# A decoder block with 32 experts on one core: down weights in two transfers, choice rows read by tile and choice, tap products ahead of state products

## What is computed

```python
D_MODEL, SEQ, N_EXPERTS, EXPERT_TOP_K, D_EXPERT = 1024, 512, 32, 2, 512
SSM_WIDTH, SSM_GROUP_DIM, SSM_STATE = 512, 16, 64        # 32 groups, 64 states each

h = rmsnorm(x, norm_mix_g); proj = h @ w_in
ya = pool_mixer(proj[..., :a_end]); yb = sgu_mixer(proj[..., a_end:b_end])
yc = s5_mixer(proj[..., b_end:c_end])
    # states = associative_scan of a complex diagonal recurrence
    # y = einsum('blgp,gcp->blgc', states, c).real + d_skip * u; gelu; gated by sigmoid(y @ glu_w)
x = x + sum(gates * (ys @ w_branch)) @ w_out
t = rmsnorm(x, norm_ffn_g)
...
for e in range(N_EXPERTS):
    y = (silu(t @ w_gate[e]) * (t @ w_up[e])) @ w_down[e]
    out = out + combine[:, e:e + 1] * y                  # two experts of a token are not zero
return rmsnorm(x + out, norm_final_g)
```

## Time and profile before

| what | us |
|---|---|
| median of 3 runs | 930.88 |
| lowest, highest | 930.44, 931.03 |
| the profiled execution | 932.56 |
| its span, first to last instruction | 930.9 |
| PE busy | 835.0 (90%) |
| DVE, ACT, POOL busy | 323.2, 195.7, 142.1 |

### The profile page before, as it was taken

How to read it: one execution, slowest core, us unless ns; L and a number is a source line. 1 busy time by engine, 2 the same in 40 slices (tenths; PEclk the granted TensorE clock), 3 DMA queues, 4 the chain that set the end, 5 groups by cost and what they waited for, 6 DMA issues and landing times.

```text
span 930.9 us, 15236 instructions
## 1 busy us (share of the span) xinstructions
PE 835.0 (90%) x5300; PEld 569.9 (61%) x5301; DVE 323.2 (35%) x604; ACT 195.7 (21%) x289; POOL 142.1 (15%) x239
## 2 busy tenths in 40 slices
PE   7999999999999999989889998899999887777850
PEld 6888888868876888885555554555555444343420
DVE  4899996731524246265101111110101101010106
ACT  5633353222432233141000000000000000000002
POOL 4341601000000000012122221122112121212100
PEclk9999999999999999999999999999999999999995
DMA  8693224523224945049999999999999999999926
GB/s 263 148 186 111 75 66 44 167 69 113 91 90 153 401 148 225 1 160 387 402 417 420 418 418 420 421 420 419 418 420 419 419 420 421 420 420 420 410 118 268
DMA packets 77949, 261.22 MB, mean 281 GB/s; under 512 B 29260, under 2 KB 30284, under 8 KB 53300
## 3 DMA queue, kind: packets, MB, share of 16 engines
q1 hardware_dynamic: 71508, 249.91, 71.1%
q0 software_dynamic: 6256, 10.75, 3.1%
q10 hardware_dynamic: 144, 0.02, 0.0%
HBM read 254.76 MB, written 14.42 MB: 289 GB/s over the span
## 4 chain that ended last, share of the span: by engine, by line
PE 71%; SPq 15%; DVE 5%; DMA 4%; issue 2%; ACT 1%; POOL 0%; DVEq 0%; POOLq 0%; ACTq 0%
PE ps L1009 35%; PE ps L436 17%; SPq L421 14%; PE ps L449 9%; DMA au<-in_exp_w_up 4%; PE ps L994 3%; PE ps L986 1%; SPq L461 1%; PE ps L442 1%; DVE pair L655 1%; DVE pair L650 1%; DVE cv L700 1%; PE ps L1120 1%; PE ps L1148 1%; PE ps L1150 1%
## 5 line engine op out<-in xcount | busy, mean ns | idle before, releaser
L436 PE MATMUL ps<-ssm,pair 128*64 128x256 f32 x1120 | 127.2, 381 | 20.2 <-DMA ssm<-in_exp_w_gate 8.9
L650 DVE TENSOR_TENSOR pair<-pair,ps 128x256 f32<-128x256 f32 x32 | 13.5, 421 | 358.5 <-PE ps L436 358.5
L436 PEld LDWEIGHTS ps<-ssm,pair 128*64 128x64 f32 x1120 | 81.3, 137 | 71.1 <-issue 28.5
L1009 PE MATMUL ps<-h_hi,w_hi 128*128 128x512 f32 x280 | 109.6, 392 | 0.0
L1427 DVE TENSOR_TENSOR w_lo<-raw,w_hi 128x1024 fp32r<-128x1024 f32 x56 | 71.3, 1274 | 110.3 <-ACT w_hi L1236 109.5
L1009 PE MATMUL ps<-h_hi,w_lo 128*128 128x512 f32 x280 | 109.0, 389 | 0.0
L1009 PE MATMUL ps<-h_lo,w_hi 128*128 128x512 f32 x280 | 108.9, 389 | 0.0
L1236 ACT CAST w_hi<-raw 128x1024 fp32r<-128x1024 f32 x59 | 61.8, 1050 | 193.2 <-PE ps L1009 193.2
L714 ACT COPY late<-ps 128x512 f32<-128x512 f32 x35 | 20.5, 586 | 317.5 <-PE ps L449 317.5
L793 POOL DMA_INDIRECT choice_rows<-late,put_now x35 | 35.7, 1021 | 319.9 <-ACT late L714 284.1
L1009 PEld LDWEIGHTS ps<-h_hi,w_hi 128*128 128x128 f32 x280 | 52.6, 188 | 11.2 <-issue 0.4
(11 more groups left out here) (319 smaller groups left out, 1099.1 us busy)
## 6 DMA issues: line engine op xcount, KB each, us to landing
ssm<-in_exp_w_gate SPq DMA_DIRECT2D x22, 2048.0 KB, 29.4
au<-in_exp_w_up SPq DMA_DIRECT2D x11, 2048.0 KB, 30.0
ssm<-in_exp_w_up SPq DMA_DIRECT2D x11, 2048.0 KB, 33.7
ssm<-in_exp_w_down SPq DMA_DIRECT2D x11, 2048.0 KB, 33.9
hl<-in_exp_w_down SPq DMA_DIRECT2D x11, 2048.0 KB, 29.8
raw<-in_w_in SPq DMA_DIRECT2D x40, 512.0 KB, 3.8
hh<-in_exp_w_gate SPq DMA_DIRECT2D x10, 2048.0 KB, 28.4
mb<-in_exp_w_up SPq DMA_DIRECT2D x10, 2048.0 KB, 30.8
```

What stands on the lines that cost most here:

```text
L436: t = nc.tensor.matmul(ps[CAP * h:CAP * (h + 1), bank, 0:HALF], rows[:, k], w[:, k, HALF * h:HALF * (h + 1)], start=k == 0, stop=k == KD - 1)
L650: nc.vector.tensor_tensor(act_cols, silu_cols, up_now, ALU.mult).then_inc(act_ready, 1)
L1009: t = nc.tensor.matmul(bank, lhs, rhs, start=k == 0 and n == 0, stop=k == 2 * count - 1 and n == 2)
```

## The change

Four things, and a tidying that makes room for their semaphores.

1. The down weights of every expert are two transfers of 1 MB, rows `[:, 0]` and `[:, 1]` of the buffer, with a semaphore each (`ew_in[w]["down"]`, `down_rest_in[w]`). `down` waits for the second between its fourth and its fifth matmul. The weights of "over" stay one transfer.
2. Ahead of the four reads of choice rows, the wait for the last scatters comes after the two counter loads and the branch. The four reads of 1 MB are eight of 512 KB, by tile and choice, and VectorE waits for each.
3. For the experts that stand outside the loop, `first_put` waits for its copy first and for the result last, without a `sem_inc` between the last wait and the scatter.
4. In the state-space outputs, the eight tap matmuls of a bank come first, then its sixteen state matmuls.
5. `done2[kind]` and `ov_done[kind]` are one semaphore each, which counts three products for a block.

```diff
-            eng.dma_start(dst, src).then_inc(signal, 16)
+            if signal is ov_w or kind != "down":
+                eng.dma_start(dst, src).then_inc(signal, 16)
+            else:
+                for h, half_in in enumerate((signal, down_rest_in[w])):
+                    eng.dma_start(dst[:, h], src[:, h]).then_inc(half_in, 16)
...
-        def down(w_, bank):
+        def down(w_, bank, pe=None, rest=0):
+
             w = slot_h[EW[w_]["down"]]
             for n, (h, j) in enumerate((h, j) for h in range(2) for j in range(2)):
+                if n == 2 and pe is not None:
+                    pe.wait_ge(down_rest_in[w_], rest)
                 for c in range(2):
...
                     sp.wait_ge(done[kind], e - SETS + 1)
-                    sp.wait_ge(done2[kind], flag + before + 1)
+                    sp.wait_ge(second_done, before * 3 + flag * DONE[kind] + 3)
                     sp.sem_inc(passed, 1)
                     weights(sp, w, kind, e, ew_in[w][kind])
...
-            for w in range(SETS):
-                sp.wait_ge(res_stored[w], USES[w] * 16)
             flag, before = second_of(sp, NE - 1)
             sp.wait_ge(second_rows, (flag + before) * 16 + 16)
             sp.sem_inc(passed, 1)
             with sp.If(n > 0):
                 sp.wait_ge(ov_res_stored, n * 16)
                 sp.sem_inc(passed, 1)
+            for w in range(SETS):
+                sp.wait_ge(res_stored[w], USES[w] * 16)
             for i in range(NT):
-                sp.dma_start(picked_rows(i), res_d.rearrange("(t r) n -> t (r n)", r=4)[i * P:(i + 1) * P, :]).then_inc(picked[i], 16)
+                for c in range(2):
+                    sp.dma_start(picked_rows(i)[:, D * c:D * (c + 1)],
+                                 res_d.rearrange("(t c h) n -> t c (h n)", c=2, h=2)[i * P:(i + 1) * P, c]).then_inc(picked[i][c], 16)
...
             for i in range(NT):
-                v.wait_ge(picked[i], 16)
                 for c in range(2):
+                    v.wait_ge(picked[i][c], 16)
...
-                gp.wait_ge(res_ready, e + 1)
-                put(res[b], e + 1, res_stored[b], put_copied, b)
+                if isinstance(e, int):
+                    gp.wait_ge(put_copied, e + 1)
+                    gp.wait_ge(res_ready, e + 1)
+                    put(res[b], None, res_stored[b], put_copied, b)
...
-                for q in range(4 * i, 4 * i + 4):
-                    outs = [bank[S * two:S * (two + 1), P * (q % 4):P * (q % 4 + 1)] for two in range(2)]
-                    halves = [slice(S * two, S * (two + 1)) for two in range(2)]
+                halves = [slice(S * two, S * (two + 1)) for two in range(2)]
+                outs = [[bank[rows, P * n:P * (n + 1)] for rows in halves] for n in range(4)]
+                for n in range(4):
                     for two in range(2):
-                        nc.tensor.matmul(outs[two], u8v[:, two * Q + q], toep[:, two * Q + q], start=True, stop=False)
-                    for two, rows in enumerate(halves):
-                        nc.tensor.matmul(outs[two], st_re[rows, q], cp_re[rows, q, 1:J + 1].rearrange("p j c -> p (j c)"), start=False, stop=False)
-                    for two, rows in enumerate(halves):
-                        t = nc.tensor.matmul(outs[two], st_im[rows, q], cp_im[rows, q, 1:J + 1].rearrange("p j c -> p (j c)"), start=False, stop=True)
+                        g = two * Q + 4 * i + n
+                        nc.tensor.matmul(outs[n][two], u8v[:, g], toep[:, g], start=n == 0, stop=False, skip_group_check=True)
+                for n in range(4):
+                    q = 4 * i + n
+                    for z, cp in ((st_re, cp_re), (st_im, cp_im)):
+                        for two, rows in enumerate(halves):
+                            t = nc.tensor.matmul(outs[n][two], z[rows, q], cp[rows, q, 1:J + 1].rearrange("p j c -> p (j c)"),
+                                                 start=False, stop=n == 3 and z is st_im, skip_group_check=True)
                 end(("y", i), t)
```

More of the change, by code:

```diff
@@ L336, in trunk @@
         passed = sem("passed")
-        picked = [sem(f"picked{i}") for i in range(NT)]
+        picked = [[sem(f"picked{i}_{c}") for c in range(2)] for i in range(NT)]
         idx_ready, ov_ready, idx_copied, ov_idx_copied = (sem(n) for n in ("idx_ready", "ov_ready", "idx_copied", "ov_idx_copied"))
@@ L348, in trunk @@
         xg_in, res_stored = per_side("xg_in"), per_side("res_stored")
-        done2 = {k: sem(f"second_{k}_done") for k in KINDS}
+        second_done, DONE = sem("second_products_done"), {kind: n + 1 for n, kind in enumerate(KINDS)}
         (xg2_in, xt2_full, xgT2_ready, silu2_ready, act2_ready, at2_full, actT2_ready, res2_ready,
@@ L497, in experts_sync @@
             flag, before = second_of(sp, NE - 2)
-            sp.wait_ge(done2["down"], flag + before + 1)
+            sp.wait_ge(second_done, (flag + before) * 3 + 3)
             sp.sem_inc(passed, 1)
@@ L534, in experts_tensor @@
             banks_free(0, 3)
-            for kind in KINDS:
-                pe.sem_inc(done2[kind], 1)
+            pe.sem_inc(second_done, 3)
             pe.sem_inc(xt2_full, 1)
@@ L571, in experts_tensor @@
             pe.wait_ge(ew_in[0]["down"], 16)
-            down(0, B_RES[0]).then_inc(done["down"], 1)
+            down(0, B_RES[0], pe, 16).then_inc(done["down"], 1)
             pe.wait_ge(xg_in[1], 16)
@@ L595, in turn @@
                     pe.wait_ge(res_ready, e - 1)
-                down(w, B_RES[w]).then_inc(done["down"], 1)
+                down(w, B_RES[w], pe, nth * 16 + 16).then_inc(done["down"], 1)
                 second_block(e, w)
@@ L606, in second_block @@
                     pe.wait_ge(xgT2_ready, before + 1)
-                    hidden(xgT2, w, "gate", B_GATE).then_inc(done2["gate"], 1)
-                    hidden(xgT2, w, "up", B_UP).then_inc(done2["up"], 1)
+                    hidden(xgT2, w, "gate", B_GATE).then_inc(second_done, 1)
+                    hidden(xgT2, w, "up", B_UP).then_inc(second_done, 1)
                     pe.wait_ge(act2_ready, before + 1)
@@ L612, in second_block @@
                     pe.wait_ge(res2_ready, before + 1)
[L613 removed]
+                    down(w, B_RES2).then_inc(second_done, 1)
             second_block(0, 0, "(j p)")
@@ L631, in over @@
                     pe.wait_ge(res_ready, NE - 1)
-                hidden(xgT, 0, "gate", B_GATE).then_inc(ov_done["gate"], 1)
-                hidden(xgT, 0, "up", B_UP).then_inc(ov_done["up"], 1)
+                hidden(xgT, 0, "gate", B_GATE).then_inc(ov_done, 1)
+                hidden(xgT, 0, "up", B_UP).then_inc(ov_done, 1)
                 pe.wait_ge(ov_act_ready, o_ + 1)
@@ L638, in over @@
                     pe.wait_ge(ov_res_ready, o_)
-                down(0, B_RES[0]).then_inc(ov_done["down"], 1)
+                down(0, B_RES[0]).then_inc(ov_done, 1)
             pe.wait_ge(ov_ready, 1)
@@ L725, in turn @@
                 with act.If(flag > 0):
-                    act.wait_ge(done2["gate"], before + 2)
+                    act.wait_ge(second_done, before * 3 + 3 + DONE["gate"])
                     nc.scalar.activation(silu, ps[:, B_GATE, 0:HALF], ACT.Silu).then_inc(silu2_ready, 1)
-                    results(res2, B_RES2, done2["down"], before + 2, res2_ready, second_rows, before * 16 + 16)
+                    results(res2, B_RES2, second_done, before * 3 + 3 + DONE["down"], res2_ready, second_rows, before * 16 + 16)
             act.wait_ge(rows0_full, 1)
@@ L743, in over @@
             def over(o_, first):
-                act.wait_ge(ov_done["gate"], o_ + 1)
+                act.wait_ge(ov_done, o_ * 3 + DONE["gate"])
                 if first:
@@ L751, in over @@
                     act.wait_ge(res_stored[0], USES[0] * 16)
-                results(res[0], B_RES[0], ov_done["down"], o_ + 1, ov_res_ready, ov_res_stored, None if first else o_ * 16)
+                results(res[0], B_RES[0], ov_done, o_ * 3 + DONE["down"], ov_res_ready, ov_res_stored, None if first else o_ * 16)
             act.wait_ge(ov_ready, 1)
@@ L789, in put @@
             def put(src, count, signal, copied, side):
-                gp.wait_ge(copied, count)
-                gp.sem_inc(passed, 1)
+                if count is not None:
+                    gp.wait_ge(copied, count)
+                    gp.sem_inc(passed, 1)
                 g.indirect_dma_start(res_d, bass.IndirectOffsetOnAxis(ap=put_now[:, side:side + 1], axis=0),
```

12 lines of the change are left out of this document (8 added, 4 removed).

## The result

| | before | changed |
|---|---|---|
| median of 5 runs, us | 930.55 | 925.88 |
| lowest, highest | 929.79, 931.03 | 925.06, 927.74 |
| profiled execution, its span | 932.56, 930.9 | 927.04, 925.3 |

The ratio is 0.9948, 95% interval 0.9930 to 0.9967, so the change gains 3.1 to 6.5 us; by the medians it is 4.7. The forecast was 925.2, a gain of 5.7, which lies inside that interval. One of the runs behind this document (`y_two`, 986.39 us at a mean granted clock of 0.84, where its other runs have about 0.98) was in a slow state and stands in no ratio.

The account below looks back on a forecast made before the run. Bound by TensorE up to 399 us, full DMA engines from 413 us, then a serial tail. Terms: 932.56 - 3.4 + 0.2 - 1.35 - 1.1 - 0.05 = 926.9, a gain of 5.7; against the median 930.88, 925.2; range 923.3 to 928.6.

Follow-up runs that it names:

- y_two: The changed kernel with the state-space outputs as taps of two banks, then states of two banks (2 alternations); ratio to the kernel before 0.9933 (0.9914 to 0.9952).

## What to carry to other kernels

Count how often TensorE alternates between products of different depth, and group them by depth where PSUM allows: each alternation had a fixed price here, and it was readable beforehand by comparing the mixed stretch with an unbroken run of the same form. Where a stage is bound by a full DMA queue, cutting transfers of 2 MB into 1 MB neither cost nor gained anything here; look for the gain in what comes before the queue fills and after it drains. Take loads and branches that don't need the awaited result out from behind the last wait of a serial tail, and measure such a small edit by its own stretch of the trace as well, since a tidying elsewhere can give the same amount back.

## What was not expected of the hardware

- The alternation between 128 and 64 rows deep costs 0.297 us, the same at 16, 12, 8, 4 and 2 alternations.
- A full queue moves 1 MB and 2 MB transfers at the same 416 to 421 GB/s, whatever their number, but eight reads of 512 KB after a pause run at 213 and 254 GB/s in their second and third microsecond and once more at 229 in the sixth, and end 1.1 us later than four reads of 1 MB (13.4 against 12.3 us).
- A scatter of 30 rows landed in 2.36 to 2.40 us in the three kernels with separate counters and in 2.90 to 3.40 in all eleven profiles with joined counters, where its last two packets start when an 8 KB load of instructions ends.
